# The prompt's compressed-branch scores, spread two by two over a mix product

## What is computed

```python
n_cmp = (lk - CMP_BLOCK) // CMP_STRIDE + 1
s = jnp.einsum('btkgd,bckd->btkgc', qg, ck) * scale
p = jnp.where(cvalid, jax.nn.softmax(jnp.where(cvalid, s, NEG), axis=-1), 0.0)
o_cmp = jnp.einsum('btkgc,bckd->btkgd', p, cv)
```

## Time and profile before

| | |
|---|---|
| median of 3 runs | 920.8 us (919.0 to 922.33) |
| the profiled execution, its own time | 921.3 us |
| its span, first to last instruction | 919.6 us |
| mean granted TensorE clock | 0.998 |
| TensorE matmul / weight load busy | 905.0 us (98%) / 750.0 us (82%) |
| VectorE / ScalarE / GpSimd busy | 553.8 us (60%) / 297.1 us (32%) / 129.7 us (14%) |
| DMA, mean | 206 GB/s |

### The profile page before, as it was taken

How to read it: one execution, slowest core, us unless ns; L and a number is a source line. 1 busy time by engine, 2 the same in 40 slices (tenths; PEclk the granted TensorE clock), 3 DMA queues, 4 the chain that set the end, 5 groups by cost and what they waited for, 6 DMA issues and landing times.

```text
span 919.6 us, 18062 instructions
## 1 busy us (share of the span) xinstructions
PE 905.0 (98%) x6588; PEld 750.0 (82%) x6588; DVE 553.8 (60%) x1538; ACT 297.1 (32%) x627; POOL 129.7 (14%) x258
## 2 busy tenths in 40 slices
PE   8999999999999999999999999999999999999998
PEld 7999778877777777888899986888777777878887
DVE  4887588876744677034258757898676546741331
ACT  3133633246733113400120346322577321233000
POOL 0430000002033262000060000000100323700000
PEclk9999999999999999999999999999999999999999
DMA  7654456317199799344465435562352998973433
GB/s 285 227 191 149 167 230 250 117 58 275 47 315 383 260 385 329 115 138 142 158 210 159 174 129 206 220 236 92 115 218 67 365 381 287 383 248 141 138 137 93
DMA packets 56794, 189.05 MB, mean 206 GB/s; under 512 B 9218, under 2 KB 22914, under 8 KB 44418
## 3 DMA queue, kind: packets, MB, share of 16 engines
q1 hardware_dynamic: 43426, 138.56, 43.0%
q0 software_dynamic: 12992, 49.16, 14.3%
q10 hardware_dynamic: 288, 0.18, 0.1%
HBM read 177.47 MB, written 18.77 MB: 213 GB/s over the span
## 4 chain that ended last, share of the span: by engine, by line
PE 84%; DVE 7%; ACT 3%; DVEq 2%; issue 2%; DMA 1%; ACTq 0%; SPq 0%
PE ps L1113 18%; PE ps L902 9%; PE ps L1435 9%; PE ps L921 9%; PE ps L1329 7%; PE ps L1447 3%; PE ps L1441 3%; PE ps L914 3%; PE ps L1308 2%; PE ps L1234 2%; PE ps L1409 2%; PE ps L1223 2%; DVE arena L2099 1%; PE ps L1201 1%; PE ps L891 1%
## 5 line engine op out<-in xcount | busy, mean ns | idle before, releaser
L1113 PE MATMUL ps<-hT,slab 128*128 128x264 f32 x736 | 174.2, 393 | 0.1
L902 PE MATMUL ps<-hT,slab 128*128 128x264 f32 (+1 forms) x736 | 171.4, 389 | 0.0
L1113 PEld LDWEIGHTS ps<-hT,slab 128*128 128x128 f32 x736 | 138.5, 192 | 30.0 <-DVEq L2253 3.2
L902 PEld LDWEIGHTS ps<-hT,slab 128*128 128x128 f32 (+1 forms) x736 | 137.7, 190 | 24.4 <-issue 1.1
L1459 ACT ACTIVATE arena<-ps 128x512 f32<-128x512 f32 (+12 forms) x138 | 64.1, 494 | 142.6 <-PE ps L1329 47.2
L1435 PE MATMUL ps<-Y,slab 128*128 128x264 f32 x384 | 85.8, 386 | 0.0
L1435 PEld LDWEIGHTS ps<-Y,slab 128*128 128x128 f32 x384 | 72.9, 190 | 12.3
L1329 PEld LDWEIGHTS ps<-arena,w 128*128 128x128 f32 x512 | 58.4, 192 | 10.0 <-issue 6.6
L1329 PE MATMUL ps<-arena,w 128*128 128x128 f32 x512 | 61.4, 278 | 0.0
L620 POOL DMA_DIRECT2D arena<-in_pages_kv_dram x64 | 33.3, 520 | 152.6 <-DVEq L2483 114.8
L629 POOL DMA_DIRECT2D arena<-in_pages_kv_dram x64 | 35.0, 547 | 98.1 <-PE ps L1329 27.0
(11 more groups left out here) (394 smaller groups left out, 1457.7 us busy)
## 6 DMA issues: line engine op xcount, KB each, us to landing
slab<-in_weights_dram SPq DMA_DIRECT2D x84, 1024.0 KB, 5.0
arena<-in_pages_kv_dram SPq DMA_DIRECT2D x64, 256.0 KB, 8.5
arena<-in_pages_kv_dram POOLq DMA_DIRECT2D x64, 256.0 KB, 6.9
arena<-in_pages_kv_dram POOLq DMA_DIRECT2D x64, 128.0 KB, 8.4
arena<-in_pages_kv_dram SPq DMA_DIRECT2D x64, 128.0 KB, 12.0
out_dram<-in_state_win_dram POOLq DMA_DIRECT2D x2, 4088.0 KB, 24.7
arena<-in_state_hgrn_dram SPq DMA_DIRECT2D x2, 2048.0 KB, 12.4
out_dram<-arena POOLq DMA_DIRECT2D x2, 2048.0 KB, 9.4
```

The lines of the kernel that those rows point to most:

```text
L902: last = mm(ps[0:job[3], n % 2, 0:LT], v[:, k, job[2]:job[2] + job[3]], hT[:, k, :], start=(k == 0), stop=(k == KD - 1))
L1113: last = mm(ps[:, bank, 0:LT], v[:, k, (d % 2) * 128:(d % 2) * 128 + 128], hT[:, k, :], start=(k == 0), stop=(k == KD - 1))
```

## The change

On TensorE alone, in the step of the scores. Before, the 16 scores stood together, and mix 11 followed as a product of its own. After, mix 11 is written out in place: for each of its 8 blocks of k one matmul, and behind it two of the scores (heads h and h + 4 of one half of the prompt). Its bank is 3 as before. The wait for the copy of mix 9 (`mixed(9)`, which was in `mix(3, after=9)`) and that for the slab come before the first of the scores; the mark of mix 11 stays on its last matmul and "s" on the last of the scores, which now is TensorE's last instruction ahead of the wait for `cp_v` "s". The other engines' programs are the same.

```diff
                 mix(2, after=8)
                 pe.wait_ge(cp_a.sem, cp_a(l, "out"))
-                for t in range(2):
-                    for h in (0, 4, 1, 5, 2, 6, 3, 7):
+                n = next(mixes)
+                mixed(9)
+                v = arrived(f"m{n // KD}{n % KD // 2}")
+                pieces = [(t, h) for t in range(2) for h in (0, 4, 1, 5, 2, 6, 3, 7)]
+                for k in range(KD):
+                    turn = mm(ps[:, 3, 0:LT], v[:, k, (n % 2) * 128:(n % 2) * 128 + 128], hT[:, k, :], start=(k == 0), stop=(k == KD - 1))
+                    for t, h in pieces[2 * k:2 * k + 2]:
                         r, j = halves[h // 4], h % 4
                         last = mm(ps[:, 4 + 2 * (h // 4) + t, j * NCP:j * NCP + NCP], Z[r, Z_NQ + j, t * 128:t * 128 + 128], ckP[r, 0:NCP], start=True, stop=True)
                 last.then_inc(cp_p.sem, cp_p.mark("s"))
-                mix(3, after=9)
+                turn.then_inc(mx_p.sem, mx_p.mark(f"m {n}"))
                 pe.wait_ge(cp_v.sem, cp_v(l, "s"))
                 mix(4)
                 mixed(11)
```

## The result

The kernel before took 920.21 us (median of 4 runs), the changed one 935.01 us (4 runs, 932.99 to 935.97): a ratio of 1.0134, interval 1.0094 to 1.0174. The change makes the kernel slower by 14.8 us. The forecast was slower by 7.6 us, 928.5, with a range up to 932.5: the direction is right, the size is half of what came.

The account below looks back on a forecast made before the run. TensorE, busy 98% of the span, was taken as the bound. Switches 1.96 + 0.1 and exposed wait 1.74 gave 3.8 us a layer, 7.6 in two, hence 928.5 us against the median, range 924.8 to 932.5.

Parts of the forecast that it names:

- The switches: TensorE, scores among mix 11: seven more height round trips of 0.29 us, cycle 0.964, 1.96 us plus 0.1 a layer.
- Rival B: Scores among mix 11: cheaper height switches, cycle 0.77 us, time 925.4, still slower; chance 0.09.
- rival C: Scores' weight loads vanish beneath mix records: not slower, cycle under 0.68 us, 920.0 at 0.45; chance 0.08.
- The exposed wait: TensorE ahead of mix(4): no product covers VectorE's work for "s" any more, a hole of 1.74 us a layer.
- The sum of the order: TensorE's path in both layers: 1.96 + 0.1 + 1.74 = 3.8 us a layer, 7.6 in two.
- The clock: Half-clock lumps of 1.7 us on mix products: left at the one before; range -1.7 to +3.4 us.
- rival D: Clock falls once more in both layers on top of A: 932.0 us; no chance of its own, A's upper part.
- A: The forecast itself, scores through mix(4): switches and exposed wait, 928.5 us; chance 0.80.
- The queues: SP's slab and POOL's page loads issued later, up to 5.6 us, landing before use: nothing, at most 1.8 us.
- Steps 3 and 4 of the sum: Earlier wait for mix 9's copy, nothing; work behind "s" ("n", ScalarE's copies) hidden by 1.5 and 1.1 us.

Follow-up runs that it names:

- two_trips: Changed kernel without the hole (mix 12 in a bank nobody waits for), scores in two groups of eight instead of eight of two: 922.7 us, ratio 1.0022.
- full_inter: Changed kernel with whole-height scores, 8 products instead of 16, one behind each block of mix 11, hole kept: 932.19 us, ratio 1.0134.
- hole_only: Kernel before with its scores still together but placed behind mix 11, so the wait for "s" is exposed: 928.38 us, ratio 1.0087.
- filled: Changed kernel with three idle products, results unused, in the hole ahead of mix(4): 929.26 us, ratio 1.0076.
- again: The changed kernel measured once more without an edit: 934.95 us over 6 runs, ratio 1.0145.
- hole_filled: hole_only with the three idle products in its hole: 926.37 us, ratio 1.0056.
- full_old: Kernel before with whole-height scores, eight together ahead of mix 11 as in its order: 925.17 us, ratio 1.005.
- half_filled: Changed kernel with one idle product instead of three in the hole ahead of mix(4): 929.14 us, ratio 1.0108.
- full_free: Changed kernel with whole-height scores behind the blocks of mix 11, and mix 12 in bank 2 ahead of the wait: 925.84 us, ratio 1.0049.

## Why the prediction was right in direction and wrong in size

1. **The switches** (step 1 of the sum): right. Cycle 0.97 for 0.964, last score to mix(4) by the forecast's own numbers. two_trips measures 0.30 us a trip for 0.29, and with whole-height scores the cycle is 0.67, the value given for no switching cost. Rival B (0.77) and rival C (under 0.68) fell with it. Against C the prediction had also set that the row groups of the halves conflict with those of the mix. That is no reason by this trace: in a mix product the weight loads, on the same 128 rows as the products, are busy 3.41 of its 3.83 us beside them (before, 271.08). What rules C out is that small products of full height add all of their own time too: a cycle of 0.67 in full_inter is 2 x 0.223 and 2 x 0.112.
2. **The exposed wait** (step 2): right. 1.92 us from the last score to mix(4) for 1.93, and hole_only, which has it alone, has its transposes 1.73 later in the layer without a clock fall there.
3. **The sum of the order**: 3.8 us a layer forecast, 3.84 in the trace of filled. In the times, with the clock's part out, the changed kernel is 8.3 over before for 7.6; the window keys are the likely difference.
4. **The clock: the step that failed.** The prediction had the mechanism and its price ("A new hole of 1.7 us a layer can bring one more in each layer"), but its sum has nothing for it: "I leave it at one", the one lump that was there before, with two more as rival D, the upper part of A. The runs show 4.7 us more of clock part in the changed kernel's first four runs than the 1.8 of the kernel before, and 5.6 in the six of again: there 7.6 of the order and 5.6 of the clock are 13.2 of the 13.8 us measured. The changed kernel's profiles have the half clock right behind the hole in four layers of four, the filled ones' (filled, hole_filled) in none of four, and the clock part is 4 to 6 us higher with the whole hole open (again, hole_only, full_inter) and 0 to 2 with it filled or never opened. The evidence set against it was too weak: a stretch at 358 with 0.8 us of holes in 2 us, the largest of 0.7, says little on a hole of 1.7 in one piece.
5. **Its size.** Even D had only two more stretches of 1.7 us. There were some three to four. Of the eight layers profiled with the whole hole open, six have mix(4) or mix 14 slow, and four have both (right behind the hole it is five of the eight, and none of the two of full_inter): 285.5 and 299.1 in the changed kernel, 285.3 and 298.9, 749.5 and 763.1 in its second profile, 281.4 and 295.0 in hole_only, 13.6 us apart each time. The kernel before has mix 14 slow in one layer of its four, and the two filled kernels in two of four, so that fall needs no open hole. Nor is every long hole followed by one: behind the six stalls of the whole-height kernels, TensorE idle for 1.2 to 1.8 us, the clock stayed at its upper level each time. Why a layer's two falls come together, and why the two profiles of the changed kernel have one at 105 us, ahead of the edited steps, where no other version but full_old had it, is left open. That falls so far from the hole are its doing isn't shown; filled, which keeps the rest of the order, loses nearly all of what the clock part had gained.
6. **The queues** (step 5): wrong in its reach. The forecast looked at the third unit of pages and took the rest from the DMA's quiet time at 305. The window keys of the last pair, issued later, in the next full stretch, have no cover at all. The kernel before already waited for them with its weight load, by 0.3 us:

```profile
PEld ps L1316 <- DMA arena<-in_win_k_dram: 0.3, 1, 0.3
```

The changed kernel's profiles have 0.9 and 1.7 us there, filled 1.2 in layer 1, half_filled 0.9, full_free 1.4 in two. As the kernel before lost 1.8 us at the same place in its second profile, this is a landing time that varies around its use by more than its slack, and the change's share in it isn't settled.

Steps 3 and 4 of the sum (mix 9's copy, "n", ScalarE's copies) cost nothing, as forecast: the transposes follow mix(4)'s end in every version that kept the wait.

## What to carry to other kernels

Before small products are spread among large ones, look at the array height of both: here every way down and back costs 0.3 us, and spreading two by two pays it eight times to hide nothing. A large product behind the small ones that feed another engine may be the cover of that engine's answer; used up as the carrier of the small ones, it leaves a hole. And where a hole opens ahead of large products, the half clock behind it belongs in the sum and not only in the range: here two holes of 1.7 us brought some 5 us of it, and idle products in the holes took that back. How often a hole brings it has to be measured at its place; six stalls of 1.2 to 1.8 us elsewhere in this study brought none.

## What was not expected of the hardware

- Three idle products in a hole of 1.66 us took 5.7 us off the time (934.95 to 929.26), though they shorten no path. The clock part went from 7.5 to 1.9.
- Such falls come in pairs 13.6 us apart, mix(4) and mix 14, in four layers of the study.
- TensorE stalled for 1.5 to 2.1 us in a straight run of products with no wait, only in the three kernels with fewer instructions ahead of it, and at the same place. It hid all that their better order had gained. A 16 KB packet of the instruction queue began 2.2 to 2.4 us before the end of each.
